# A one-layer decoder step on one core: what ScalarE waits for between two expert products, and how the output is finished and scaled

## The chip, the cores and the metric

The kernel runs on one core of one Trainium2 chip. The metric is the device time of one execution in microseconds (us). The engines are called by the names that the profile uses: PE (TensorE matmul), PEld (its weight loads), DVE (VectorE), ACT (ScalarE), POOL (GpSimd), SP (SyncE, which issues the weight stream). ACTq is the part of ACT that issues DMAs.

## What is computed

288 tokens (256 of a prompt, 8 x 4 of running samples) of width 2048 go through one layer: adaLN modulation, a mixer of an RG-LRU branch and a pooling branch, and an expert layer with 16384 experts. The part that matters here is the end of the expert layer and of the model:

```python
act = jax.nn.gelu(jnp.einsum('td,ted->te', xb, eu[ib]))   # the u product
return jnp.einsum('te,ted->td', wb * act, ev[ib])          # the v product
...
x = x + g2[:, None] * peer(...)                            # residual with a gate
y = rmsnorm(x, final_g)                                    # over the 2048 features
```

The kernel computes both expert products densely: all 16384 experts for all 288 tokens, with the chosen experts' gates written into a mostly zero matrix that is multiplied onto the gelus.

## The kernel before

Features lie on partitions, as 16 chunks of 128; tokens are columns, so a full activation is 128 x 16 x 288. Every float32 weight tile of 128 x 2048 (a unit) comes through one stream into four `raw` buffers and is split in two: ACT rounds it to `w_hi` (line 984 or 992, the functions `hi` and `hi_next`), DVE subtracts to get `w_lo` (lines 484 and 491, `lo` and `lo_next`). Both have two buffers (`SPL = 2`). PE then does three products for a unit: `w_hi` with the high and with the low part of the activation (the hi part of a unit), and `w_lo` with the high part (its lo part). PE signals `pe_hi` after a hi part and `pe_unit` after a unit. ACT may overwrite a `w_hi` buffer after `pe_hi` of the unit two before.

The program runs through the modulation and mixer, the queries, 128 u units and then 128 v units. In the u part ACT turns each unit's result into gelus and stores them, in 16 groups of eight units, to a scratch tensor in DRAM (`store_gelus`, line 1146). The staging tile of these gelus is the same memory as `acc`, in which the v part later sums. In the v part, group g multiplies the gelus and gates of eight units by eight v tiles; each v unit k of a group makes two feature chunks, c = 2k (complete with `vhalf_done`) and c = 2k + 1 (complete with `pe_unit`). They lie in four PSUM banks in turn, and DVE adds them to `acc[:, c]` (line 930; line 928 copies in the first group). Between these, DVE and ACT prepare the next group: `gated` multiplies gelus by gates, ACT rounds (line 1173), DVE subtracts (line 887). ACT also loads gates (line 1164) and gelus (line 1168) of a later group.

Order on each engine is the order in which the code is written; engines meet only through semaphores. At the passage from u to v, ACT stores the last group of gelus, waits until all 16 stores have landed (`gelu_out`), loads gelus 1, gates 2 and gelus 2, and only then rounds the weights of the second v unit. DVE waits for the same stores before its first instruction of the v part.

The last group is unrolled. In it DVE finishes chunks as well: for each unit it makes `w_lo` of the next, adds both chunks, and then runs `finish` for both: `residual` (lines 717, 720, 722) puts the gated sum onto `x`, `add_square` (lines 726, 727) adds the square to a running sum in `rstd`. ACT in this group only rounds weights. After the last chunk DVE copies the sum (line 955), PE adds over partitions (line 1271), ACT takes the square root (line 997), DVE inverts it (line 523) and scales 16 chunks by `final_g` and by the inverse (line 958). After every four chunks SP writes a quarter of the output (line 413).

Of the kernel before, what the change touches and what calls it, by code (L numbers as in the profile page):

```python
# [9 lines left out]
ALU = mybir.AluOpType  # L10
ACT = mybir.ActivationFunctionType
# [3 lines left out]
P = 128  # L15
D = 2048
DC = D // P
SEQ = 256
NB, NS = 8, 4
T = SEQ + NB * NS  # L20
# [41 lines left out]
EG = 8  # L62
NG = P // EG
# [46 lines left out]
NQ = 4  # L110
# [8 lines left out]
def v_unit(g):  # L119
    return V0 + EG * g  # L120
# [36 lines left out]
class Chain:  # L157
# [12 lines left out]
    def link(self, ins):  # L170
        self.done(ins)
        self.wait()
# [26 lines left out]
def hybrid_step(nc, w_stream, vecs_d, c_d, hist_d, x_d, lruw_d, poolw_d, keys_d,  # L199
                o_y, o_conv, o_lru, o_pool):  # L200
    ctx = ExitStack()
    with ctx:
        def sb(name, shape, dt=F, scope=None):
            return (scope or ctx).enter_context(nc.sbuf_tensor(name, shape, dt))

        def sem(name):
            return ctx.enter_context(nc.semaphore(name))
# [7 lines left out]
        x = sb("x", [P, DC, T])  # L215
# [8 lines left out]
        rstd = sb("rstd", [P, 2, T])  # L224
# [16 lines left out]
        acc = sb("acc", [P, DC, T])  # L241
# [5 lines left out]
        def bank(b, n=512, at=0):  # L247
            return ps[:, b * 512 + at:b * 512 + at + n]

        def vec(name):  # L250
            o, w = VOFF[name]
            return vecs[:, o:o + w]
# [118 lines left out]
        gelu_out = [sem("gelu_out0"), sem("gelu_out1")]  # L371
# [4 lines left out]

        vbank_free = [sem(f"vbank{b}_free") for b in range(4)]
        out_ready = sem("out_ready")
        out_sem = sem("out_sem")
        dve_steps, act_steps, pool_steps = sem("dve_steps"), sem("act_steps"), sem("pool_steps")  # L380

# [90 lines left out]
        def _(dve):  # L472
            ch = Chain(dve, dve_steps)
            link = ch.link
            V = nc.vector

            def lo(u):
                if plain(u):
                    return
                s, old = place(u) % SPL, split_before(u)  # L480
                dve.wait_ge(hi_ready, place(u) + 1)
                if old is not None:
                    dve.wait_ge(pe_unit, old + 1)
                V.tensor_tensor(w_lo[:, s, :], raw[:, u % RAW, :], w_hi[:, s, :].bitcast(F), ALU.subtract).then_inc(lo_ready, 1)  # L484
# [212 lines left out]
            for u in range(2 * DC, O0):  # L697
                lo(u + 1)
                kind = ORDER[u - 1]
                if kind[0] == "z" and kind[1] < 16:  # L700
                    n = kind[1]
# [5 lines left out]
                k = ORDER[u - 3]  # L707
# [6 lines left out]
            def residual(c, src, m):  # L714

                xs = x[:, c, SEQ:T].rearrange("p (b t) -> p b t", t=NS)
                V.scalar_tensor_tensor(out=x[:, c, 0:SEQ], in0=src[:, 0:SEQ], scalar=mod[:, m, c, 0:1],
                                       in1=x[:, c, 0:SEQ], op0=ALU.mult, op1=ALU.add)
                tmp = rstd[:, 1, 0:NB * NS].rearrange("p (b t) -> p b t", t=NS)
                link(V.tensor_tensor(tmp, src[:, SEQ:T].rearrange("p (b t) -> p b t", t=NS),  # L720
                                     mod[:, m, c, 1:].unsqueeze(2).to_broadcast([P, NB, NS]), ALU.mult))
                return V.tensor_tensor(xs, xs, tmp, ALU.add)

            def add_square(c, square):

                link(V.tensor_tensor(square, x[:, c, :], x[:, c, :], ALU.mult))
                link(V.tensor_tensor(rstd[:, 0, :], rstd[:, 0, :], square, ALU.add))
# [16 lines left out]
            for u in range(Q0 + 3, Q0 + 8):  # L744
                lo(u + 1)
                kind, n = QORDER[u - Q0 - 1]
# [128 lines left out]
            def gated(tile, g, k, par, turn):  # L875

                if k == 0:
                    dve.wait_ge(gate_in[par], turn)
                    dve.wait_ge(gelu_in[par], turn)
                src = gel_in(g)  # L880
                at_least(dve, gw_ready, tile - 1)
                V.tensor_tensor(prod[:, k % 2, :].rearrange("p (c t) -> p c t", t=TCH), src[:, k, :].rearrange("p (c t) -> p c t", t=TCH),  # L882
                                gates_in[:, par, :, k * TCH:(k + 1) * TCH], ALU.mult).then_inc(prod_done, 1)

            def gated_low(tile, k, par):
                dve.wait_ge(gwhi_ready, tile + 1)
                V.tensor_tensor(gw_lo[:, par, k, :], prod[:, k % 2, :], gw_hi[:, par, k, :].bitcast(F),
                                ALU.subtract).then_inc(gw_ready, 1)

            steps, left = choose(), 0.0  # L890
            for n in range(P):
                now[0] = n
                lo(M0 + n + 1)
                if GATE0_AT <= n < GATE0_AT + EG:
                    k = n - GATE0_AT
# [10 lines left out]
                    left -= cost  # L906
            assert next(steps, "end") == "end" and made["ones", NBT - 1] + 2 < GATE0_AT - 3

            for h in range(2):
                dve.wait_ge(gelu_out[h], 16 * (NG // 2))  # L910

            def v_group(lo_of, tile, par, turn, unit, units, uses, last=None):

                start = isinstance(uses, int) and uses == 0
                if not start:
                    for b in range(4):
                        dve.wait_ge(vbank_free[b], uses)
                for k in range(EG):
                    lo_of(k)
                    for j in TILES[k] if last is None else ():  # L920
                        gated(tile + j, 2 - par, j, par, turn)
                    dve.wait_ge(vhalf_done, units + (k + 1))
                    for h in range(2):
                        c = 2 * k + h
                        if h == 1:
                            dve.wait_ge(pe_unit, unit + (k + 1))
                        if start:
                            n = V.tensor_copy(acc[:, c, :], bank(2 + c % 4, T))
                        else:
                            n = V.tensor_tensor(acc[:, c, :], acc[:, c, :], bank(2 + c % 4, T), ALU.add)  # L930
                        n.then_inc(vbank_free[c % 4], 1)
                    for j in TILES[k] if last is None else ():
                        gated_low(tile + j, j, par)
                    if last:
                        last(2 * k)
                        last(2 * k + 1)

            v_group(lambda k: lo(v_unit(0) + k + 1), EG, 1, 16, v_unit(0), 0, 0)
            with dve.Fori(0, NG // 2 - 1) as i:
                for j in range(2):  # L940
# [5 lines left out]
            def finish(c):  # L946

                dve.wait_ge(vbank_free[c % 4], (NG - 1) * DC // 4 + c // 4 + 1)
                link(residual(c, acc[:, c, :], 5))
                add_square(c, prod[:, 0, :])  # L950

            dve.wait_ge(gw_ready, NG * EG)
# [1 line left out]
            v_group(lambda k: lo(v_unit(g) + k + 1) if k < EG - 1 else None, 0, 0, 0, v_unit(g), g * EG, g * DC // 4, last=finish)  # L954
            V.tensor_copy(prod[:, 1, :], rstd[:, 0, :]).then_inc(sq_ready, 1)
            inv_std(5, rstd[:, 0, :])
            for c in range(DC):
                n = V.scalar_tensor_tensor(out=acc[:, c, :], in0=x[:, c, :], scalar=vec("final")[:, c:c + 1],  # L958
                                           in1=rstd[:, 0, :], op0=ALU.mult, op1=ALU.mult)
                if c % (DC // NQ) == DC // NQ - 1:  # L960
                    n.then_inc(out_ready, 1)


        @block.scalar
        def _(act):
# [9 lines left out]
            def hi(u):  # L975

                if plain(u):
                    return
                s, old = place(u) % SPL, split_before(u)
                act.wait_ge(raw_in[u % RAW], 16 * (u // RAW + 1))  # L980
                if old is not None:
                    act.wait_ge(pe_hi, place(old) + 1)
                    low_made(old)
                nc.scalar.activation(w_hi[:, s, :], raw[:, u % RAW, :], ACT.Copy).then_inc(hi_ready, 1)  # L984
# [95 lines left out]
            for u in range(2 * DC, O0):  # L1080
# [5 lines left out]
                if kind[0] == "z" and kind[1] >= 16:  # L1086
                    n = kind[1]
# [5 lines left out]
                k = ORDER[u]  # L1093
# [109 lines left out]
                if GATE0_AT <= n < GATE0_AT + EG:  # L1203
                    gated_high(n - GATE0_AT, n - GATE0_AT, 0)

            for h in range(2):
                act.wait_ge(gelu_out[h], 16 * (NG // 2))
            act.wait_ge(pe_unit, V0)
            load_gelus(1, gel_in(1), 1)

            def v_group(hi_of, tile, load, par):

                act.wait_ge(gw_ready, tile)
                load()
                for k in range(EG):
                    hi_of(k)
                    for j in TILES[k]:
                        gated_high(tile + j, j, par)

            def load_next(g, h):  # L1220
                return lambda: (load_gates(g, h), load_gelus(g, gel_in(2 - h), h))

            v_group(lambda k: hi(v_unit(0) + k + 1), EG, load_next(2, 0), 1)
            with act.Fori(0, NG // 2 - 2) as i:
                for j in range(2):
                    g = 1 + j

                    def load():
                        if j == 0:
                            load_gates(i * 2 + 3, 1)  # L1230
                            load_gelus(i * 2 + 3, gel_in(1), 1)
                        else:
                            load_gates(i * 2 + 4, 0)
                            load_gelus(i * 2 + 4, gel_in(2), 0)
                    v_group(lambda k: hi_next(v_unit(g), i, 2 * EG, k), i * (2 * EG) + (g + 1) * EG, load, j)
# [1 line left out]
            v_group(lambda k: hi(v_unit(g) + k + 1), (g + 1) * EG, load_next(g + 2, 1), 0)  # L1237
            g = NG - 2
            v_group(lambda k: hi(v_unit(g) + k + 1), (g + 1) * EG, lambda: None, 1)
            for k in range(EG - 1):  # L1240
                hi(v_unit(NG - 1) + k + 1)

            stats(5, rstd[:, 0, :], D, 6)

# [265 lines left out]
```

## Time and profile before

| | |
|---|---|
| median of 3 runs | 2378.15 us (2377.18 to 2379.47) |
| the profiled execution, its own time | 2377.09 us |
| its span, first to last instruction | 2375.1 us |
| PE busy | 2247.8 us, 95% |
| DVE busy | 1381.4 us, 58% |
| ACT busy | 831.8 us, 35% |
| mean granted TensorE clock | 0.971 |

The span is some 2 us shorter than the execution's own time, which includes what lies around the first and the last instruction. Busy shares are means over stages with different limits. In a timeline row the first number is the start in us from the span's start, the second the duration; what stands in brackets is how long the engine sat idle before the row and who ended that.

### The profile page before, as it was taken

The page shows a single profiled execution, that of the slowest core. Times are in us where ns is not written, and L with a number is a line of the kernel's source. Part 1 is how long each engine was busy: PE and PEld are TensorE (multiplying, and loading weights), DVE is VectorE, ACT ScalarE, POOL GpSimd, SP SyncE. Part 2 cuts the span into 40 slices and gives each one's busy share as a digit, 9 for nine tenths or more (in the row PEclk, how much of TensorE's full clock was granted, in tenths as well). Part 3 has the DMA queues.
Part 4 walks back from the last instruction along what each step waited for, and adds up shares of the span by engine and source line. Part 5 has one row for each costly group of instructions (what it writes and reads, how often), then busy time and mean ns, then how long its engine had stood idle before and what let it go on. Part 6 is the DMA issues. An engine that isn't in the chain of part 4 may idle for free.

```text
span 2375.1 us, 38461 instructions
## 1 busy us (share of the span) xinstructions
PE 2247.8 (95%) x16551; PEld 2129.1 (90%) x16551; DVE 1381.4 (58%) x1909; ACT 831.8 (35%) x727; POOL 18.6 (1%) x60
## 2 busy tenths in 40 slices
PE   5599968979999999999999999899999999999997
PEld 0198747968899999999999999899999999999996
DVE  3336546663478886677663334365665566656668
ACT  0222243222333333445543333333333333333331
POOL 0000000000000000000000000000000000000000
PEclk8799988989999999999999999999999999999998
DMA  9967766447644555555555557655555655555542
GB/s 404 380 260 299 269 277 246 161 160 277 228 172 180 184 182 196 199 200 221 212 211 200 188 192 254 213 209 206 210 199 206 233 213 201 199 205 210 199 159 79
DMA packets 105843, 515.93 MB, mean 217 GB/s; under 512 B 8448, under 2 KB 45696, under 8 KB 46464
## 3 DMA queue, kind: packets, MB, share of 16 engines
q1 hardware_dynamic: 59616, 430.35, 48.8%
q10 hardware_dynamic: 45968, 82.17, 9.4%
q8 instruction: 90, 1.47, 0.2%
q0 software_dynamic: 144, 1.73, 0.2%
q14 instruction: 25, 0.20, 0.0%
HBM read 471.92 MB, written 41.99 MB: 216 GB/s over the span
## 4 chain that ended last, share of the span: by engine, by line
PE 90%; DMA 4%; DVE 3%; ACT 1%; issue 1%; ACTq 0%; SPq 0%; DVEq 0%
PE ps L1258 17%; PE ps L1259 16%; PE ps L1264 16%; PE ps L1425 12%; PE ps L1424 11%; PE ps L1432 11%; DMA raw<-in_w_stream_dram 4%; PE ps L1395 3%; PE ps L1283 2%; PE ps L1271 1%; PE ps L1372 0%; DVE mix L502 0%; ACT w_hi L984 0%; DVE act_lo L511 0%; DVE acc L958 0%
## 5 line engine op out<-in xcount | busy, mean ns | idle before, releaser
L1258 PE MATMUL ps<-act_hi,w_hi 128*128 128x288 f32 x2944 | 806.0, 301 | 28.1 <-ACT w_hi L984 14.5
L1259 PE MATMUL ps<-act_lo,w_hi 128*128 128x288 f32 x2944 | 799.6, 298 | 0.0
L484 DVE TENSOR_TENSOR w_lo<-raw,w_hi 128x2048 fp32r<-128x2048 f32 x188 | 430.6, 2291 | 391.2 <-ACT w_hi L984 372.2
L1258 PEld LDWEIGHTS ps<-act_hi,w_hi 128*128 128x128 f32 x2944 | 559.9, 190 | 45.9 <-issue 40.8
L1424 PE MATMUL ps<-gw_hi,w_hi 128*128 128x288 f32 x2048 | 554.4, 297 | 7.7 <-ACT w_hi L984 7.7
L1259 PEld LDWEIGHTS ps<-act_lo,w_hi 128*128 128x128 f32 x2944 | 559.5, 190 | 0.1
L1425 PE MATMUL ps<-gw_lo,w_hi 128*128 128x288 f32 x2048 | 554.7, 298 | 0.0
L984 ACT ACTIVATE w_hi<-raw 128x2048 fp32r<-128x2048 f32 x192 | 367.4, 1914 | 230.6 <-DMA raw<-in_w_stream_dram 103.7
L1264 PE MATMUL ps<-act_hi,w_lo 128*128 128x288 f32 x2944 | 420.8, 295 | 0.1
L1264 PEld LDWEIGHTS ps<-act_hi,w_lo 128*128 128x128 f32 x2944 | 401.3, 189 | 0.3 <-DVE w_lo L484 0.3
L1424 PEld LDWEIGHTS ps<-gw_hi,w_hi 128*128 128x128 f32 x2048 | 386.3, 189 | 7.9 <-ACT w_hi L984 7.9
L1425 PEld LDWEIGHTS ps<-gw_lo,w_hi 128*128 128x128 f32 x2048 | 387.9, 189 | 0.0
L992 ACT ACTIVATE w_hi<-raw 128x2048 fp32r<-128x2048 f32 x120 | 229.9, 1916 | 206.5 <-PE ps L1425 84.2
L491 DVE TENSOR_TENSOR w_lo<-raw,w_hi 128x2048 fp32r<-128x2048 f32 x124 | 283.5, 2286 | 32.1 <-ACT w_hi L992 27.9
L1432 PE MATMUL ps<-gw_hi,w_lo 128*128 128x288 f32 x2048 | 293.9, 296 | 0.0
L1432 PEld LDWEIGHTS ps<-gw_hi,w_lo 128*128 128x128 f32 x2048 | 280.2, 188 | 0.0
L930 DVE TENSOR_TENSOR acc<-acc,ps 128x288 f32<-128x288 f32 x240 | 108.4, 454 | 285.9 <-PE ps L1432 285.9
L1141 ACT ACTIVATE acc<-ps 128x288 f32<-128x288 f32 x128 | 52.6, 411 | 495.5 <-PE ps L1264 495.5
L1173 ACT ACTIVATE gw_hi<-prod 128x288 fp32r<-128x288 f32 x128 | 55.7, 444 | 378.4 <-DVE prod L882 377.9
L1283 PE MATMUL ps<-raw,csil 128*32 128x512 f32 x768 | 119.9, 720 | 51.8 <-DMA raw<-in_w_stream_dram 45.2
L1283 PEld LDWEIGHTS ps<-raw,csil 128*32 128x32 f32 x768 | 18.1, 116 | 127.1 <-DMA raw<-in_w_stream_dram 100.0
L1156 ACT ACTIVATE mix<-ps 128x512 f32<-128x512 f32 x72 | 70.7, 1092 | 2.1 <-PE ps L1395 2.1
(166 smaller groups left out, 937.6 us busy)
## 6 DMA issues: line engine op xcount, KB each, us to landing
raw<-in_w_stream_dram SPq DMA_DIRECT2D x408, 1024.0 KB, 4.9
gelus<-acc ACTq DMA_DIRECT2D x16, 1152.0 KB, 6.6
gates_dense<-mix ACTq DMA_DIRECT2D x18, 1024.0 KB, 4.5
gates_in<-gates_dense ACTq DMA_DIRECT2D x16, 1152.0 KB, 6.6
act_hi<-gelus ACTq DMA_DIRECT2D x15, 1152.0 KB, 11.5
x<-in_x_dram ACTq DMA_DIRECT2D x1, 2304.0 KB, 15.5
out_dram<-acc SPq DMA_DIRECT2D x4, 576.0 KB, 2.8
out_dram<-mix POOLq DMA_DIRECT2D x1, 1692.0 KB, 8.7
```

Source lines behind the costliest of these rows:

```text
L484: V.tensor_tensor(w_lo[:, s, :], raw[:, u % RAW, :], w_hi[:, s, :].bitcast(F), ALU.subtract).then_inc(lo_ready, 1)
L491: V.tensor_tensor(w_lo[:, s, :], raw[:, n % RAW, :], w_hi[:, s, :].bitcast(F), ALU.subtract).then_inc(lo_ready, 1)
L930: n = V.tensor_tensor(acc[:, c, :], acc[:, c, :], bank(2 + c % 4, T), ALU.add)
L984: nc.scalar.activation(w_hi[:, s, :], raw[:, u % RAW, :], ACT.Copy).then_inc(hi_ready, 1)
L992: nc.scalar.activation(w_hi[:, place(n) % SPL, :], raw[:, n % RAW, :], ACT.Copy).then_inc(hi_ready, 1)
L1258: mm(bank(b, T), w_hi[:, s, w], act_hi[:, c, :], start=c == 0, stop=False)
L1259: n = mm(bank(b, T), w_hi[:, s, w], act_lo[:, c, :], start=False, stop=False)
L1264: n = mm(bank(b, T), w_lo[:, s, w], act_hi[:, c, :], start=False, stop=c == DC - 1)
L1283: n = mm(bank(4 + m % 2)[CPAD * b:CPAD * (b + 1), :], csil[:, k, :], raw[:, u % RAW, b * 512:(b + 1) * 512], start=k == 0, stop=k == DC - 1)
L1424: mm(bank(2 + b, T), w_hi[:, s, w], gw_hi[:, par, e, :], start=e == 0, stop=False)
L1425: n = mm(bank(2 + b, T), w_hi[:, s, w], gw_lo[:, par, e, :], start=False, stop=False)
L1432: n = mm(bank(2 + b, T), w_lo[:, s, w], gw_hi[:, par, e, :], start=False, stop=e == EG - 1)
```

## The change

Three edits.

1. At the passage, ACT's wait for all gelu stores becomes a wait for the first store of odd groups (`gelu_out[1]` at 16), which is that of group 1, the one that it loads next. The wait for all stores moves behind ACT's first v group, ahead of the loop. On DVE it moves from ahead of the v part to just ahead of the first copy into `acc`.
2. In the last group DVE calls `finish` for a chunk right behind that chunk's own sum, not for both chunks behind both sums. `finish` signals ACT through a new semaphore, `xnew_ready`, once the chunk's new `x` is written.
3. ACT, in the last group, scales each finished chunk by `final_g` into `acc` (a Copy with a scale per partition) and signals `xg_ready`. At the very end DVE multiplies four quarters of 128 x 1152 by the inverse, in place of 16 chunks of 128 x 288 with two factors.

```diff
-            for h in range(2):
-                dve.wait_ge(gelu_out[h], 16 * (NG // 2))
-
             def v_group(lo_of, tile, par, turn, unit, units, uses, last=None):
...
                         if start:
+                            if c == 0:
+                                for b in range(2):
+                                    dve.wait_ge(gelu_out[b], 16 * (NG // 2))
                             n = V.tensor_copy(acc[:, c, :], bank(2 + c % 4, T))
                         else:
                             n = V.tensor_tensor(acc[:, c, :], acc[:, c, :], bank(2 + c % 4, T), ALU.add)
                         n.then_inc(vbank_free[c % 4], 1)
+                        if last:
+                            last(c)
                     for j in TILES[k] if last is None else ():
                         gated_low(tile + j, j, par)
-                    if last:
-                        last(2 * k)
-                        last(2 * k + 1)
-
...
                 dve.wait_ge(vbank_free[c % 4], (NG - 1) * DC // 4 + c // 4 + 1)
-                link(residual(c, acc[:, c, :], 5))
+                residual(c, acc[:, c, :], 5).then_inc(xnew_ready, 1)
+                dve.wait_ge(xnew_ready, c + 1)
                 add_square(c, prod[:, 0, :])
...
-            for c in range(DC):
-                n = V.scalar_tensor_tensor(out=acc[:, c, :], in0=x[:, c, :], scalar=vec("final")[:, c:c + 1],
-                                           in1=rstd[:, 0, :], op0=ALU.mult, op1=ALU.mult)
-                if c % (DC // NQ) == DC // NQ - 1:
-                    n.then_inc(out_ready, 1)
+            for q in range(NQ):
+                n = DC // NQ
+                c = slice(q * n, (q + 1) * n)
+                dve.wait_ge(xg_ready, (q + 1) * n)
+                V.tensor_tensor(acc[:, c, :], acc[:, c, :], rstd[:, 0, :].unsqueeze(1).to_broadcast([P, n, T]),
+                                ALU.mult).then_inc(out_ready, 1)
...
-            for h in range(2):
-                act.wait_ge(gelu_out[h], 16 * (NG // 2))
+            act.wait_ge(gelu_out[1], 16)
             act.wait_ge(pe_unit, V0)
             load_gelus(1, gel_in(1), 1)
...
             v_group(lambda k: hi(v_unit(0) + k + 1), EG, load_next(2, 0), 1)
+            for h in range(2):
+                act.wait_ge(gelu_out[h], 16 * (NG // 2))
...
-            for k in range(EG - 1):
-                hi(v_unit(NG - 1) + k + 1)
+            for k in range(EG):
+                if k < EG - 1:
+                    hi(v_unit(NG - 1) + k + 1)
+                for c in (2 * k, 2 * k + 1):
+                    act.wait_ge(xnew_ready, c + 1)
+                    nc.scalar.activation(acc[:, c, :], x[:, c, :], ACT.Copy, scale=vec("final")[:, c:c + 1]).then_inc(xg_ready, 1)
```

How ACT's instructions stand at the passage, before. The first row is the last unit's gelu, `gelus<-acc` the last store, the last row the weights of the second v unit; semaphores that a row waits for stand in brackets.

```order
L1141 ACTIVATE acc<-ps 128x288 [waits pe_unit]
L1146 DMA gelus<-acc 128x2304 [waits bank1_free,bank0_free]
L1168 DMA act_hi<-gelus 128x2304 [waits pe_unit,gelu_out1,gelu_out0]
L1164 DMA gates_in<-gates_dense 128x18x128 [waits gw_ready]
L1168 DMA act_hi<-gelus 128x2304
L984 ACTIVATE w_hi<-raw 128x2048 [waits lo_ready,pe_hi,raw_in1]
```

The same place now (line numbers are one higher):

```order
L1142 ACTIVATE acc<-ps 128x288 [waits pe_unit]
L1147 DMA gelus<-acc 128x2304 [waits bank1_free,bank0_free]
L1169 DMA act_hi<-gelus 128x2304 [waits pe_unit,gelu_out1]
L1165 DMA gates_in<-gates_dense 128x18x128 [waits gw_ready]
L1169 DMA act_hi<-gelus 128x2304
L985 ACTIVATE w_hi<-raw 128x2048 [waits lo_ready,pe_hi,raw_in1]
```

No row moved: one semaphore is gone from the first load, and the other is waited for at a lower value. All three loads still stand ahead of the weights.

How ACT's program ends, before: the weights of the last three units, and the square root.

```order
L984 ACTIVATE w_hi<-raw 128x2048 [waits lo_ready,pe_hi,raw_in1]
L984 ACTIVATE w_hi<-raw 128x2048 [waits lo_ready,pe_hi,raw_in2]
L984 ACTIVATE w_hi<-raw 128x2048 [waits lo_ready,pe_hi,raw_in3]
L997 ACT_TABLE_LOAD
L997 ACTIVATE rstd<-ps,epsc 128x288 [waits stat_ready]
```

And now:

```order
L985 ACTIVATE w_hi<-raw 128x2048 [waits lo_ready,pe_hi,raw_in2]
L1247 ACTIVATE acc<-x,vecs 128x288 [waits xnew_ready] x2
L985 ACTIVATE w_hi<-raw 128x2048 [waits lo_ready,pe_hi,raw_in3]
L1247 ACTIVATE acc<-x,vecs 128x288 [waits xnew_ready] x4
L998 ACT_TABLE_LOAD
L998 ACTIVATE rstd<-ps,epsc 128x288 [waits stat_ready]
```

Two scaled copies, each with a wait for DVE, stand between the weights of one unit and of the next; the table load now stands behind the last of them.

How DVE's instructions of one unit stand in the last group, before:

```order
L484 TENSOR_TENSOR w_lo<-raw,w_hi 128x2048 [waits pe_unit,hi_ready,dve_steps]
L930 TENSOR_TENSOR acc<-acc,ps 128x288 [waits vhalf_done]
L930 TENSOR_TENSOR acc<-acc,ps 128x288 [waits pe_unit]
L717 SCALAR_TENSOR_TENSOR x<-acc,mod,x 128x256 [waits vbank0_free]
L720 TENSOR_TENSOR rstd<-acc,mod 128x32
L722 TENSOR_TENSOR x<-x,rstd 128x32 [waits dve_steps]
L726 TENSOR_TENSOR prod<-x 128x288 [waits dve_steps]
L727 TENSOR_TENSOR rstd<-rstd,prod 128x288 [waits dve_steps]
L717 SCALAR_TENSOR_TENSOR x<-acc,mod,x 128x256 [waits vbank1_free,dve_steps]
```

And now, up to the second chunk's residual:

```order
L485 TENSOR_TENSOR w_lo<-raw,w_hi 128x2048 [waits pe_unit,hi_ready,dve_steps]
L931 TENSOR_TENSOR acc<-acc,ps 128x288 [waits vhalf_done]
L718 SCALAR_TENSOR_TENSOR x<-acc,mod,x 128x256 [waits vbank0_free]
L721 TENSOR_TENSOR rstd<-acc,mod 128x32
L723 TENSOR_TENSOR x<-x,rstd 128x32 [waits dve_steps]
L727 TENSOR_TENSOR prod<-x 128x288 [waits xnew_ready]
L728 TENSOR_TENSOR rstd<-rstd,prod 128x288 [waits dve_steps]
L931 TENSOR_TENSOR acc<-acc,ps 128x288 [waits pe_unit,dve_steps]
L718 SCALAR_TENSOR_TENSOR x<-acc,mod,x 128x256 [waits vbank1_free]
```

The second sum moved behind the first chunk's residual and square; `w_lo` of the next unit is still the first of a unit's instructions.

## Rows read from the trace of the kernel before

**Rows 1.** The page's chain that ended last, by engine

```profile
PE 90%; DMA 4%; DVE 3%; ACT 1%; issue 1%; ACTq 0%; SPq 0%; DVEq 0%
```

**Rows 2.** Timeline of ACT at the passage (start, duration, engine, line, what)

```profile
1524.81 0.35 ACTq L1146 DMA_DIRECT2D gelus<-acc  x1
1530.45 0.35 ACTq L1168 DMA_DIRECT2D act_hi<-gelus  x1
1530.84 0.45 ACTq L1164 DMA_DIRECT2D gates_in<-gates_dense  x1
1531.32 5.01 ACTq L1168 DMA_DIRECT2D act_hi<-gelus  x1
1536.45 1.91 ACT L984 ACTIVATE w_hi<-raw 128x2048 fp32r<-128x2048 f32 x1 [11.72 <-issue]
```

**Rows 3.** Timeline of PE at the passage

```profile
1528.41 2.29 PE L1432 MATMUL ps<-gw_hi,w_lo 128*128 128x288 f32 x16
...
1538.41 0.61 PE L1424 MATMUL ps<-gw_hi,w_hi 128*128 128x288 f32 x1 [7.71 <-ACT w_hi L984]
...
1545.42 2.29 PE L1432 MATMUL ps<-gw_hi,w_lo 128*128 128x288 f32 x16
```

**Rows 4.** Timeline of ACT one group later: a gelu load behind a gate load

```profile
1581.42 2.37 ACTq L1168 DMA_DIRECT2D act_hi<-gelus  x1
```

**Rows 5.** Stretches: us; busy of PE, PEld, DVE, ACT, POOL; clock; DMA; GB/s

```profile
226.30:230.70 4.40, 0.06 (x4) 0.00 (x0) 0.02 (x1) 1.91 (x1) 0.00 (x0) 0.94 1.00 421
230.80:233.80 3.00, 3.00 (x13) 3.00 (x14) 2.73 (x2) 1.91 (x1) 0.00 (x0) 0.53 1.02 431
...
262.80:264.50 1.70, 0.22 (x5) 0.17 (x2) 1.70 (x3) 0.73 (x1) 0.00 (x0) 1.00 1.00 352
...
2367.60:2374.30 6.70, 0.00 (x0) 0.00 (x0) 4.30 (x11) 0.00 (x0) 0.00 (x0) 0.50 0.85 352
```

**Rows 6.** Timeline of PE in the last group: lo parts of its units 0 and 1

```profile
2309.39 2.30 PE L1432 MATMUL ps<-gw_hi,w_lo 128*128 128x288 f32 x16
...
2315.81 2.30 PE L1432 MATMUL ps<-gw_hi,w_lo 128*128 128x288 f32 x16
```

**Rows 7.** Timeline of DVE in the last group, its units 0 and 1

```profile
2310.66 0.46 DVE L930 TENSOR_TENSOR acc<-acc,ps 128x288 f32<-128x288 f32 x1 [2.26 <-PE ps L1432]
2311.73 0.46 DVE L930 TENSOR_TENSOR acc<-acc,ps 128x288 f32<-128x288 f32 x1 [0.61 <-PE ps L1432]
...
2312.94 0.46 DVE L726 TENSOR_TENSOR prod<-x 128x288 f32<-128x288 f32 x1
...
2313.93 0.48 DVE L717 SCALAR_TENSOR_TENSOR x<-acc,mod,x 128x256 f32<-128x256 f32 x1
...
2315.76 2.29 DVE L484 TENSOR_TENSOR w_lo<-raw,w_hi 128x2048 fp32r<-128x2048 f32 x1
2317.97 0.81 DVE L930 TENSOR_TENSOR acc<-acc,ps 128x288 f32<-128x288 f32 x2
```

**Rows 8.** Timeline of ACT: an activation of 288 columns and the next instruction

```profile
1492.66 0.44 ACT L1173 ACTIVATE gw_hi<-prod 128x288 fp32r<-128x288 f32 x1
1492.99 1.91 ACT L984 ACTIVATE w_hi<-raw 128x2048 fp32r<-128x2048 f32 x1
```

**Rows 9.** Timeline of ACT at the end: table load and square root

```profile
2343.67 1.28 ACT L997 ACT_TABLE_LOAD   x1
2362.43 0.50 ACT L997 ACTIVATE rstd<-ps,epsc 128x288 f32<-128x288 f32 x1 [17.47 <-PE ps L1271]
```

**Rows 10.** Timeline of DVE at the end: last sum, copy, scaling

```profile
2356.66 0.46 DVE L930 TENSOR_TENSOR acc<-acc,ps 128x288 f32<-128x288 f32 x1 [0.54 <-PE ps L1432]
...
2360.70 0.31 DVE L955 COPY prod<-rstd 128x288 f32<-128x288 f32 x1
...
2364.95 6.96 DVE L958 SCALAR_TENSOR_TENSOR acc<-x,vecs,rstd 128x288 f32<-128x288 f32 x16
```

**Rows 11.** Timeline of DVE earlier: a quarter of 1152 columns by a broadcast factor

```profile
490.65 1.36 DVE L499 TENSOR_TENSOR mix<-x,rstd 128x1152 f32<-128x1152 f32 x1
```

More of the change, by code:

```diff
@@ L378, in hybrid_step @@
         out_ready = sem("out_ready")
+        xnew_ready, xg_ready = sem("xnew_ready"), sem("xg_ready")
         out_sem = sem("out_sem")
```

## The prediction, made before the changed kernel had run

> **What bounds the kernel now.** I read the chain that ended last, then the timelines of ACT, PE and DVE where the diff touches them. The chain is PE for 90% of the span [rows 1], and nearly all of that is matmuls behind matmuls, which the change doesn't touch. So only two places can move the time: the passage, where PE stands still, and the end, where PE is done and DVE, ACT and the output DMA stand in the chain.
>
> At the passage PE ends the first v unit 2.14 us into its lo part, at 1530.6, and stands for 7.71 us until ACT has rounded the second unit's weights [rows 3]. ACT is free of gelus when it issues the last store at 1524.81, issues the next DMA at 1530.45 (when the store has landed), and then sits 5.01 us in the issue of gelus 2; only then come the weights, at 1536.45 [rows 2]. The stall has a tail: the next hi part takes 1538.41 to 1545.42, 7.01 us [rows 3], against 2/3 of a 6.42 us unit, 4.28 [rows 6]: 2.73 us more, at the lower granted clock. The passage thus costs 10.4 us.
>
> In the last group a unit takes PE 6.42 us [rows 6]. DVE is as full: `w_lo` (2.21 from its start to the next instruction), two sums and two finishes, 6.59 us in all [rows 7]. ACT has slack there.
>
> **Edit 1, the passage.** The wait for the store goes, and what is late next is the issue of gelus 2, which stays ahead of the weights. With a gate load alone ahead, such an issue takes 2.37 us [rows 4]; with gelus 1 ahead as well, 5.01 [rows 2]. So one 1152 KB transfer ahead costs 2.64. Now the last store (also 1152 KB) is ahead too: 2.37 + 2 x 2.64 = 7.65. The three issues now start right behind the store's, at 1525.2; gelus 2 at about 1526.0 (0.35 and 0.45 for the two before it), held to 1533.7. I take 1534.0, since the store also shares the engines with a weight load. Before it ended at 1536.33. The stall shrinks by 2.3 us, to 5.4. Bounds: no gain, if the loads are held until the store has landed all the same; 7.7, if the store and gelus 1 don't hold the issue at all.
>
> The clock's tail: a stretch of 4.4 us without work on PE, earlier in the trace, is followed by 3.0 us at a granted clock of 0.53, in which 13 matmuls run [rows 5] where 6.42 / 48 = 0.134 each would give 22: 9 x 0.134 = 1.2 us lost. After 7.71 us it is 2.73. For 5.4 us I take 2.0, so 0.7 is gained, between 0 and 1.5. **Edit 1: 3.0 us gained** (0 to 10.4). DVE's moved wait costs nothing: its first copy into `acc` comes after the weights in any case, and the store has landed by then. The wait behind ACT's first v group comes some 50 us (8 x 6.42) after the store.
>
> **Edits 2 and 3, the last group.** ACT's program now has two scaled copies between the weights of one unit and of the next. So the weights of unit k + 1 wait for the new `x` of chunk 2k - 1, which DVE makes after unit k - 1 is complete; and DVE's `w_lo` waits for those weights and stands ahead of the next sums. That closes a ring through both engines. One turn, from the sum of a unit's second chunk: 1.21 until its `x` is written (2311.73 to 2312.94); the copy; 1.91 for the weights [rows 2]; 0.04 to DVE; 2.21 for `w_lo`; 2.20 for sum and finish of the first chunk (2311.73 to 2313.93) [rows 7]. The copy: an activation of 288 columns holds ACT 0.33 [rows 8], one with a pointer operand runs 0.50 [rows 9]; I take 0.40. Sum: 7.97 us, against PE's 6.42: 1.55 more per unit, once the slack is used.
>
> The slack, in the clock times of before: the first sum is at 2310.66 [rows 7], the second 2.20 later at 2312.86, its `x` at 2314.07, the copy ends at 2314.47, weights of unit 2 are ready at 2316.38. PE wants them when unit 1 ends, at 2315.81 + 2.14 = 2317.95 [rows 6]: in time. One turn on, unit 3's weights are ready at 2324.35, wanted at 2324.37: just in time. Unit 4's at 2332.32, wanted at 2330.79: 1.53 late. Each further turn adds 1.55, so unit 7 starts 1.53 + 3 x 1.55 = 6.2 us late. Behind it DVE makes `w_lo` of unit 7 (from 2356.27), then chunks 12 to 15 at 2.20 each, and reaches the copy of the sum at 2367.3, where it was at 2360.70 [rows 10]: **6.6 us lost**. With a copy of 0.33 or 0.50 the turn is 7.90 or 8.07 and the loss 6.1 or 7.2.
>
> **Edit 3, the tail.** Sixteen scalings take 6.96 us, so the first quarter is out after four of them, about 1.8 us [rows 10]. A quarter by a broadcast factor takes 1.36 [rows 11], so the first write starts 0.45 sooner and the last quarter is done some 1.8 sooner. But the four writes fill 0.85 of the DMA engines' 6.7 us [rows 5], so they can close up by 1.0 at most: 1.45. I take **1.4 gained** (0.5 to 1.8). The table load, until now far ahead of its use [rows 9], moves behind the last copy. From the last sum ACT needs 1.21 + 0.45 + 1.28 = 2.9 us to have it; DVE and PE need 2.20 + 1.73 = 3.9 to bring ACT its input (1.73 from DVE's copy to the square root [rows 9, 10]). So it hides with 1 us to spare.
>
> The Trainium skill (ScalarE: Activation LUTs, What ACT_TABLE_LOAD costs) gives a switch of tables 1.28 us and a drain of 1.38 on top, about 2.66 in all. The row has the 1.28; nothing stood behind it that would show a drain. By the page the table would be there 4.3 us after the last sum, 0.4 after the input, and the sum below would be 0.4 higher.
>
> **The sum.** -3.0 + 6.6 - 1.4 = +2.2 us. On the profiled execution's 2377.09 that is 2379.3. It lies 1.06 under the median of 2378.15, so the time to expect of a median is 2380.3. A measurement of this kernel can tell about 0.2%, 4.8 us, so this is no change that it can show: two opposite effects of several us.
>
> **The rivals.**
> *The issue isn't held.* If gelus 2 is taken without the queue having to drain, the weights come at about 1526.8, before PE wants them: no stall, no low clock, 10.4 gained in place of 3.0. Net -5.2: 2373.0. For it: the store itself takes 0.35 to issue [rows 2]. Against it: every gelu load behind a gate load is held over 2 us, and longer with more ahead [rows 2, 4]. The Trainium skill (DMA: Bandwidth & Descriptors, Queues, rings and completion order) says that an engine takes a ring's descriptors in order. By that rule the gate load can't pass the store, and this rival falls.
> *The hold ends no earlier.* If the loads' data moves only once the store has landed, ACT is free at 1536.3 as before, and the end alone counts: +5.2, 2383.3, slower. For it: no row shows a load issued behind a store in flight. It decides where edit 1 gains under 0.4.
> *The clock falls in the last group.* Slower, too: PE now stands four times for 1.5 us. An earlier stretch of 1.7 us in which PE worked 0.22 kept 1.00 [rows 5]; if a row of such stalls doesn't, a unit costs 1.2 to 2.7 more. Up to 1.55 that hides in the ring's turn, except in the last unit; at 2.73 it is 3 x 1.18 + 2.73 = 6.3 more, 2386.6. It passes the bound from about 1.8 a unit.
> *The ring doesn't form.* If the weights don't wait for the copies, PE keeps its pace, chunk 14 is finished while chunk 15 is summed, the copy of the sum is 0.7 earlier and the tail 1.4: -3.0 - 2.1 = -5.1, 2373.1. The order of ACT's rows speaks against it.
>
> **How the numbers follow.** My forecast has 0.70 (2377.5 to 2383), the issue not held 0.08, the hold as long as before 0.10, the clock 0.08, no ring 0.04. The range leaves out the two fast rivals and the clock at its worst: 2375.5 to 2384.0. Faster by over 0.2%: the two fast rivals, less the part that ends short of it, 0.10. Slower: the hold as before, half of the clock, and a small edge of my forecast where the copy takes 0.5 and the tail gains little, 0.20. Within: 0.70.
>
> **What would show it.** At the passage: the issue of gelus 2 held about 8 us and ending near 1534, PE's stall near 5.4, and a low clock after it. In the last group: weights on ACT no longer released by PE but behind the scaled copies; PE with stalls of about 1.5 before units 4 to 7; DVE idle about 1.5 before each `w_lo`. At the end: four instructions of about 1.36, writes nearly back to back, the table load clear of the square root. I am wrong if PE shows no stalls in the last group, or if the one at the passage is gone or unchanged.

## The result: slower by 0.22%, in three parts

The changed kernel takes 2385.26 us (median of 13 runs, 2382.49 to 2387.95), the kernel before 2380.61 us (median of 13 runs, 2377.18 to 2382.59). The ratio is 1.0022, with a 95% interval of 1.0013 to 1.0030: some 5.2 us slower. (The ratios here are estimated from all runs and need not equal the quotient of the two medians, which differ by 4.65.) The prediction took 0.2% for the least that a measurement of this kernel can tell; the interval, 0.0009 to either side, is narrower than that and excludes a ratio of 1. The forecast was +2.2 us and 2380.3 us, with a range of 2375.5 to 2384.0. The direction of each part was right, the sum was not, and the time lies outside the range.

One table holds nearly everything that follows. Each profiled execution is cut at two instructions of DVE: the first sum of the last group and the copy of the sum of squares. A is the time from the issue of the last gelu store to that first sum (the passage and the v groups), B from there to the copy (the last group), C from the copy to the end of the span (the tail). The rows of before are [rows 2, 7, 10], with its span (2375.13 to the hundredth); the others are worked out in the same way from their own timelines.

| kernel | A | B | C | ratio to before |
|---|---|---|---|---|
| before | 785.85 | 50.04 | 14.44 | |
| changed | 783.23 | 59.03 | 13.16 | 1.0022 (1.0013 to 1.0030) |
| e1, passage alone | 783.89 | 50.04 | 14.44 | 0.9987 (0.9978 to 0.9996) |
| e2, end alone | 784.80 | 59.05 | 13.16 | 1.0034 (1.0023 to 1.0044) |
| e3, no copies on ACT | 783.21 | 50.39 | 14.41 | 0.9988 (0.9979 to 0.9997) |
| e4, copies one unit later | 783.48 | 50.39 | 13.16 | 0.9991 (0.9982 to 1.0000) |
| e5, gates loaded last | 775.30 | 59.03 | 13.13 | 0.9988 (0.9979 to 0.9997) |
| e8, loads behind the weights | 780.09 | 59.02 | 13.15 | 0.9995 (0.9986 to 1.0004) |
| e9, sums first | 782.70 | 57.73 | 13.15 | a single run |
| e6, three things mended | 776.58 | 49.65 | 13.15 | 0.9954 (0.9941 to 0.9968) |

So the change gives 2.62 us in A, takes 8.99 in B and gives 1.28 in C: +5.1 us in the two profiled executions. (Their spans differ by 8.3; the other 3.2 lie ahead of the last gelu store, in code that the change doesn't touch.)

**The passage (A).** ACT's timeline at the passage, against [rows 2]:

```profile
1527.97 0.35 ACTq L1147 DMA_DIRECT2D gelus<-acc  x1
1528.41 0.39 ACTq L1169 DMA_DIRECT2D act_hi<-gelus  x1
1528.84 1.29 ACTq L1165 DMA_DIRECT2D gates_in<-gates_dense  x1
1530.16 7.49 ACTq L1169 DMA_DIRECT2D act_hi<-gelus  x1
1537.77 1.91 ACT L985 ACTIVATE w_hi<-raw 128x2048 fp32r<-128x2048 f32 x1 [9.89 <-issue]
```

The wait for the store is gone, and the time is spent in the issue of gelus 2 instead: 7.49 us where it was 5.01. The weights start 9.8 us after the store's issue, where it was 11.6. PE's timeline shows the rest, against [rows 3]:

```profile
1531.56 2.29 PE L1439 MATMUL ps<-gw_hi,w_lo 128*128 128x288 f32 x16
...
1539.74 0.61 PE L1431 MATMUL ps<-gw_hi,w_hi 128*128 128x288 f32 x1 [5.88 <-ACT w_hi L985]
```

The stall is 5.88 us, where it was 7.71. The stretches say what the clock did (length; busy us of PE, PEld, DVE, ACT, POOL with instructions; granted clock; DMA share; GB/s):

```profile
1533.85:1539.74 5.89, 0.01 (x2) 0.01 (x1) 0.02 (x1) 1.91 (x1) 0.00 (x0) 0.77 1.08 340
1539.74:1546.00 6.26, 6.26 (x33) 6.26 (x34) 5.41 (x8) 2.62 (x3) 0.00 (x0) 0.67 0.90 346
```

The granted clock fell during the stall, as before, and 33 matmuls took 6.26 us, 1.8 more than 33 x the 0.134 that one takes at the upper level.

**The last group (B).** DVE's timeline over one unit, against [rows 7]:

```profile
2313.53 0.45 DVE L931 TENSOR_TENSOR acc<-acc,ps 128x288 f32<-128x288 f32 x1
2314.01 0.48 DVE L718 SCALAR_TENSOR_TENSOR x<-acc,mod,x 128x256 f32<-128x256 f32 x1
...
2314.86 0.46 DVE L727 TENSOR_TENSOR prod<-x 128x288 f32<-128x288 f32 x1
...
2317.29 2.29 DVE L485 TENSOR_TENSOR w_lo<-raw,w_hi 128x2048 fp32r<-128x2048 f32 x1 [1.48 <-ACT w_hi L985]
2319.50 0.45 DVE L931 TENSOR_TENSOR acc<-acc,ps 128x288 f32<-128x288 f32 x1
...
2321.82 0.45 DVE L931 TENSOR_TENSOR acc<-acc,ps 128x288 f32<-128x288 f32 x1
```

ACT's timeline beside it:

```profile
2314.86 0.54 ACT L1247 ACTIVATE acc<-x,vecs 128x288 f32<-128x288 f32 x1 [1.79 <-DVE x L723]
2315.30 1.90 ACT L985 ACTIVATE w_hi<-raw 128x2048 fp32r<-128x2048 f32 x1
2320.83 0.54 ACT L1247 ACTIVATE acc<-x,vecs 128x288 f32<-128x288 f32 x1 [3.63 <-DVE x L723]
```

That is the ring. DVE sums the second chunk of a unit at 2313.53 and has its `x` at 2314.86; ACT copies and reaches the weights at 2315.30; DVE, idle for 1.48 us, makes `w_lo` at 2317.29 and sums the next second chunk at 2321.82: 8.29 us a turn of the ring, against 6.42 on PE. PE's timeline shows what that does to it (a few matmuls of the group; in brackets the stall):

```profile
2325.55 0.40 PE L1431 MATMUL ps<-gw_hi,w_hi 128*128 128x288 f32 x1 [0.49 <-ACT w_hi L985]
...
2333.84 0.40 PE L1431 MATMUL ps<-gw_hi,w_hi 128*128 128x288 f32 x1 [1.60 <-ACT w_hi L985]
...
2342.13 0.40 PE L1431 MATMUL ps<-gw_hi,w_hi 128*128 128x288 f32 x1 [1.60 <-ACT w_hi L985]
...
2350.42 0.40 PE L1431 MATMUL ps<-gw_hi,w_hi 128*128 128x288 f32 x1 [1.61 <-ACT w_hi L985]
```

These are the stalls before units 3 to 6; the one before unit 7 is 1.60. Over the whole stretch B the granted clock stays at 1.00:

```profile
2311.20:2370.23 59.03, 47.29 (x344) 45.88 (x342) 47.60 (x103) 19.83 (x23) 0.00 (x0) 1.00 0.14 52
```

**The tail (C).** DVE's and ACT's ends, against [rows 9, 10]:

```profile
2369.80 1.28 ACT L998 ACT_TABLE_LOAD   x1
2371.96 0.50 ACT L998 ACTIVATE rstd<-ps,epsc 128x288 f32<-128x288 f32 x1 [0.88 <-PE ps L1278]
```

```profile
2370.23 0.31 DVE L955 COPY prod<-rstd 128x288 f32<-128x288 f32 x1
...
2374.48 5.16 DVE L961 TENSOR_TENSOR acc<-acc,rstd 128x1152 f32<-128x1152 f32 x4
```

From the copy to the first scaling it is 4.25 us in both kernels; the scaling itself takes 5.16 us where it took 6.96, and the span ends 1.28 sooner after the copy. The four writes now run at 0.96 of the DMA engines, where it was 0.85 [rows 5]:

```profile
2376.60:2382.60 6.00, 0.00 (x0) 0.00 (x0) 3.04 (x3) 0.00 (x0) 0.00 (x0) 0.50 0.96 393
```

### The profile page after: what moved, and what is told of

It is laid out like the page before. It is cut to its first block, busy times and chain, and to the rows that moved or that the text cites. A ratio compares the mean times of both kernels' runs of the same rounds, so it can differ in the third digit from the quotient of the medians.

```text
span 2383.4 us, 38467 instructions
## 1 busy us (share of the span) xinstructions
PE 2251.8 (94%) x16551; PEld 2130.6 (89%) x16551; DVE 1380.6 (58%) x1897; ACT 840.1 (35%) x743; POOL 18.8 (1%) x60
## 4 chain that ended last, share of the span: by engine, by line
PE 88%; DVE 5%; DMA 4%; ACT 2%; issue 1%; ACTq 1%; DVEq 0%; SPq 0%
PE ps L1265 17%; PE ps L1266 16%; PE ps L1271 16%; PE ps L1432 11%; PE ps L1431 11%; PE ps L1439 11%; DMA raw<-in_w_stream_dram 4%; PE ps L1402 3%; PE ps L1290 2%; ACT w_hi L985 1%; DVE w_lo L485 1%; PE ps L1278 1%; PE ps L1379 0%; DVE mix L503 0%; DVE x L718 0%
## 6 DMA issues: line engine op xcount, KB each, us to landing
act_hi<-gelus ACTq DMA_DIRECT2D x15, 1152.0 KB, 11.5
```

## Experiments

### The two halves apart

e1 has the passage edit alone, e2 the end alone.

```diff
 e1 (the kernel before):
-            for h in range(2):
-                act.wait_ge(gelu_out[h], 16 * (NG // 2))
+            act.wait_ge(gelu_out[1], 16)
 (DVE's wait moved to its first copy into acc, ACT's behind its first v group)
 e2 (the changed kernel): the same lines the other way round
```

> The kernel before with the passage edit alone. In the trace of the changed kernel the stall at the passage is 5.88 us against 7.71, and the low clock behind it costs some 0.8 us less. Theory (the store in front of the three loads holds their issue, so only a part of the stall goes): 2.6 us faster than before, ratio 0.9989, stall on PE between 5.4 and 6.4 us. Rival (the gain shows only because the stages ahead ran otherwise in that execution): stall within 0.3 us of 7.7, no gain. Rival (the issue isn't held): no stall, 10.4 us faster, ratio 0.9956.

Measured: ratio 0.9987, 3.1 us faster (the interval allows 1.0 to 5.2). PE's stall:

```profile
1541.31 0.61 PE L1425 MATMUL ps<-gw_hi,w_hi 128*128 128x288 f32 x1 [6.15 <-ACT w_hi L984]
```

B and C are those of before to the hundredth. The theory holds: a part of the stall goes, not all of it. The stall is 1.56 us shorter than in the profile of before, and A is 1.96 shorter; the other 0.4 lies behind the stall, at the low clock.

> The kernel before with the edits of the last group and the tail alone. Theory (a ring through ACT and DVE of 8.3 us a unit against PE's 6.42): PE stalls of about 1.6 us before units 4 to 7 and a smaller one before unit 3, copy of the sum about 9 us later, writes done 1.2 us sooner after it; 7.8 us slower than before, ratio 1.0033. Rival (the two parts are not independent, and what the passage gives is taken back at the end): between 4 and 6 us slower.

Measured: ratio 1.0034, 8.1 us slower (5.5 to 10.5). B is 59.05, C 13.16, those of the changed kernel; the waits of the stretch have the same five PE stalls (engine, for whom: us in total, times, longest):

```profile
DVE w_lo L485 <- ACT w_hi L985: 8.9, 6, 1.5
...
PE ps L1430 <- ACT w_hi L985: 6.9, 5, 1.6
```

The halves are independent: 0.9987 x 1.0034 = 1.0021, against 1.0022 of both. The interval (5.5 to 10.5 us) alone would not rule out the upper end of the rival's 4 to 6; B and C in the trace do. One thing beside: with the passage of before, A is 784.80 here and 785.85 in the profile of before, so the same code at the same place differs by 1 us between executions: 0.2 in the stall (7.49 here, 7.71 there), the rest behind it. By the table, the passage edit is worth 0.9 to 3.2 us, depending on which two executions one compares.

### What closes the ring

e3 takes ACT's copies away; e4 keeps them and puts them one unit later; e9 keeps them in place and restores the order of the sums.

```diff
 e3 (the changed kernel):
-            for k in range(EG):
-                if k < EG - 1:
-                    hi(v_unit(NG - 1) + k + 1)
-                for c in (2 * k, 2 * k + 1): ... (wait and scaled copy)
+            for k in range(EG - 1):
+                hi(v_unit(NG - 1) + k + 1)
 (and the sixteen scalings of before on DVE)
 e4 (the changed kernel):
+            def scaled(k): ... (the waits and copies of chunks 2k and 2k + 1)
             for k in range(EG):
                 if k < EG - 1:
                     hi(v_unit(NG - 1) + k + 1)
-                for c in (2 * k, 2 * k + 1): ...
+                if k:
+                    scaled(k - 1)
+            scaled(EG - 1)
 e9 (the changed kernel): finish(2k) and finish(2k + 1) behind both sums
```

> The changed kernel without the scaled copies on ACT: weights alone on ACT in the last group, sixteen scalings on DVE at the end as before; each chunk is still finished behind its own sum. Theory (the ring through ACT is what costs): no PE stall in the last group, a DVE turn of 2.21 + 2 x 2.32 = 6.85 us, copy of the sum 0.3 us later than before relative to the group's start; with the passage 2.3 us faster than before, ratio 0.9990. Rival (the new order of finishing costs, since each residual now waits for its own sum to end): PE stalls stay, 5 us or more slower than before.

Measured: ratio 0.9988, 2.9 us faster than before. PE waits for nobody in the last group, and DVE runs without a gap; two turns of its timeline:

```profile
2317.04 2.29 DVE L485 TENSOR_TENSOR w_lo<-raw,w_hi 128x2048 fp32r<-128x2048 f32 x1
2319.25 0.45 DVE L931 TENSOR_TENSOR acc<-acc,ps 128x288 f32<-128x288 f32 x1
2321.56 0.45 DVE L931 TENSOR_TENSOR acc<-acc,ps 128x288 f32<-128x288 f32 x1
2323.89 2.29 DVE L485 TENSOR_TENSOR w_lo<-raw,w_hi 128x2048 fp32r<-128x2048 f32 x1
```

A turn is 6.85 us (2317.04 to 2323.89), as expected, and B 50.39, 0.35 over before. The copies close the ring, not the order of finishing.

> The changed kernel with ACT's scaled copies one unit later: the copies of a unit's two chunks stand behind the weights of the unit after next, not ahead of them. Nothing is left out. Theory (the ring is closed by the place of the copies, not by their cost): no PE stall in the last group, DVE turn 6.85 us, the tail 1.2 us shorter; 3.5 us faster than before, ratio 0.9985. Rival (ACT's or DVE's added work itself is too much, or the copies disturb DVE): a turn over 7.2 us and PE stalls, slower than before.

Measured: ratio 0.9991, 2.1 us faster than before, with an interval (0.0 to 4.3 us) that takes in the 3.5 expected. In the trace B is 50.39 and C 13.16: the full gain of the tail, and the loss of the last group gone. The same sixteen copies run on ACT, and its weights are released by PE again. The copies of chunks 0 and 1 now stand ahead of the weights of unit 3; in the changed kernel they stood ahead of those of unit 2:

```profile
2315.42 0.54 ACT L1245 ACTIVATE acc<-x,vecs 128x288 f32<-128x288 f32 x1 [1.79 <-DVE x L723]
2317.16 1.92 ACT L985 ACTIVATE w_hi<-raw 128x2048 fp32r<-128x2048 f32 x1 [1.20 <-PE ps L1437]
```

So the copies cost nothing by themselves. What cost 8.6 us (59.03 to 50.39) was their place ahead of the next weights.

> The changed kernel with both sums ahead of both finishes again; ACT's scaled copies stay where they are. Theory (the ring is closed by the copies' place; the order of finishing only sets its length): PE stalls stay in the last group, a turn of 0.73 + 1.83 + 0.84 + 0.44 + 1.91 + 0.04 + 2.21 = 8.0 us against 8.29, stalls of about 1.3 us, 1.5 to 2 us less lost than in the changed kernel. Rival (finishing behind each chunk's own sum closes the ring): no PE stall in the last group.

Measured in a single run, so the trace counts more than its time. The stalls stay, a little shorter, by the waits of the last group:

```profile
DVE w_lo L485 <- ACT w_hi L986: 8.9, 6, 1.5
...
PE ps L1432 <- ACT w_hi L986: 6.2, 5, 1.4
```

`w_lo` stands at 2316.16, 2324.20, 2332.24: a turn of 8.04, as worked out. B is 57.73, 1.3 less than in the changed kernel, where 1.5 to 2 were expected. The start takes some of it back. DVE now sums both chunks of unit 0 before it finishes either, and stands 0.61 us for the second:

```profile
2310.69 0.46 DVE L931 TENSOR_TENSOR acc<-acc,ps 128x288 f32<-128x288 f32 x1 [0.61 <-PE ps L1440]
...
2316.16 2.29 DVE L485 TENSOR_TENSOR w_lo<-raw,w_hi 128x2048 fp32r<-128x2048 f32 x1 [1.48 <-ACT w_hi L986]
```

From the group's first sum to this `w_lo` it takes 6.54 us, where it was 6.09: 0.45 more. The five turns that follow give 1.24, and the last unit gives 0.51 (10.98 from its `w_lo` to the copy of the sum, where it was 11.49). The order of finishing sets the ring's length, and doesn't close it.

### What holds ACT at the passage

e5 exchanges two DMAs, e8 puts the weights ahead of both.

```diff
 e5 (the changed kernel):
-            v_group(..., EG, load_next(2, 0), 1)
+            v_group(..., EG, lambda: (load_gelus(2, gel_in(2), 0), load_gates(2, 0)), 1)
 e8 (the changed kernel), in ACT's first v group:
                 for k in range(EG):
                     hi_of(k)
+                    if k == 0:
+                        load()
```

> The changed kernel with two DMAs at the passage exchanged: gelus 2 is loaded ahead of gates 2. Nothing is left out. Theory (what holds ACT is the DMA right behind a gate load, whose 512 B pieces are made only as the queue drains; with the gate load last nobody stands behind it): the weights of the second v unit start within 4 us of the store's issue (9.7 in the changed kernel), PE's stall there is under 1 us and the clock stays; 7 us faster than the changed kernel, 2.5 us faster than before, ratio 0.9990. Rival (the queue takes only so many transfers at a time, whatever their pieces): ACT is held 6 us or more all the same, stall on PE over 3 us, no gain on the changed kernel.

Measured: ratio 0.9988 to before, 2.9 us faster, while B is still 59.03. ACT's timeline:

```profile
1527.41 0.35 ACTq L1147 DMA_DIRECT2D gelus<-acc  x1
1527.86 2.29 ACTq L1169 DMA_DIRECT2D act_hi<-gelus  x2
1530.18 0.85 ACTq L1165 DMA_DIRECT2D gates_in<-gates_dense  x1
1531.15 1.92 ACT L985 ACTIVATE w_hi<-raw 128x2048 fp32r<-128x2048 f32 x1 [3.83 <-issue]
```

The same four transfers are taken in 3.6 us, and the weights start 3.7 us after the store's issue. PE has no stall at the passage at all, and the clock stays. A is 775.30, 7.9 less than in the changed kernel and 10.5 less than before: the whole passage, as it was priced. The rival falls: the queue takes four transfers in 3.6 us. What is held for long is the DMA behind a gate load. Why that is so (by the expectation, pieces that are made only as the queue drains) this run doesn't show.

> The changed kernel with the weights of the second v unit put ahead of the loads of gates 2 and gelus 2 (gelus 1 stays ahead). Theory: the weights start about 1.5 us after the store's issue and PE doesn't stall at this unit, whatever holds the loads; but ACT is then held by gelus 2 until some 10 us after the store's issue and DVE's first gated products wait for gelus 1, so the third unit's weights come about when PE wants them: stall there between 0 and 2 us. 6 to 7.5 us faster than the changed kernel, ratio to before 0.9990 to 0.9995. Rival (what PE saves at the second unit it loses at the third): stalls of 4 us or more there, no gain.

Measured: ratio 0.9995; A is 780.09, 3.1 less than in the changed kernel, half of what was expected. ACT's and PE's timelines:

```profile
1527.11 1.91 ACT L985 ACTIVATE w_hi<-raw 128x2048 fp32r<-128x2048 f32 x1 [1.10 <-issue]
1527.13 1.05 ACTq L1165 DMA_DIRECT2D gates_in<-gates_dense  x1
1528.21 10.60 ACTq L1169 DMA_DIRECT2D act_hi<-gelus  x1
1538.86 0.78 ACT L1174 ACTIVATE gw_hi<-prod 128x288 fp32r<-128x288 f32 x2 [9.83 <-issue]
1539.54 1.89 ACT L985 ACTIVATE w_hi<-raw 128x2048 fp32r<-128x2048 f32 x1
```

```profile
1541.49 0.42 PE L1434 MATMUL ps<-gw_hi,w_hi 128*128 128x288 f32 x1 [3.08 <-ACT w_hi L985]
```

The second unit's weights are early, and the hold falls on the third unit's: 10.60 us, longer than the 7.49 in the changed kernel. This is the rival's mechanism at three quarters of its size (3.08 for 4 or more), and some gain is left. Why the hold is 3 us longer here wasn't tried, but the trace shows what else ran. From 1535 to 1538, inside the hold, a weight tile takes the DMA engines: SP's queue q1 moves 1.04 MB and ACT's queue q10 only 0.15 (queue: packets, MB, share of 16 engines).

```profile
q1 hardware_dynamic: 139, 1.04, 86.0%
q10 hardware_dynamic: 269, 0.15, 17.1%
```

In the changed kernel's trace the same 3 us, in which its hold ends, have no packet of q1:

```profile
q10 hardware_dynamic: 1291, 1.00, 102.8%
```

The size fits; a run without that tile, which would show it, wasn't made.

### A version that takes both

```diff
 e6 (the changed kernel): e5's order of loads, e4's place of the copies, and
-                        if last:
+                        if last and k == EG - 1:
                             last(c)
...
+                    if last and k < EG - 1:
+                        last(2 * k)
+                        last(2 * k + 1)
```

> The changed kernel with three things mended: gates 2 loaded behind gelus 2, the scaled copies one unit later on ACT, and both sums ahead of both finishes again, except in the last unit. Theory (the parts add up): passage 10 us less than before, copy of the sum 0.4 us earlier, tail 1.2 us shorter: 11.6 us faster than before, ratio 0.9951, no PE stall in the last group and a DVE turn of 6.6 us. Rival (the hold on ACT stays): 4 us faster than before, ratio 0.9983.

Measured: 2367.43 us against 2379.33 of before, ratio 0.9954 (0.9941 to 0.9968): 11 us faster by the ratio. A is 776.58 (a stall of 1.05 us is left before the third unit, whose weights wait behind ACT's gated products), B 49.65, 0.39 under before, C 13.15. The parts add up: -9.3, -0.4 and -1.3. PE's waits in the last stretch are down to the one for DVE's sum:

```profile
PE ps L1286 <- DVE prod L958: 4.1, 1, 4.1
```

## Why the prediction was wrong

**Edit 1: the stall was priced well, the clock's part came out by luck.** Forecast: 3.0 us gained, 2.3 in the stall and 0.7 in the low clock behind it; trace 2.6, of which 1.8 in the stall; e1 3.1. The issue of gelus 2 was forecast to be held about 8 us and to end 9.2 after the store's issue; it was held 7.49 and ended 9.7 after. The pricing of a transfer ahead at 2.64 us from two rows was good enough (the sum of 7.65 stands against 6.3 to 7.8 in the five executions with this order of loads); not foreseen was that the gate load's own issue is held too (1.29 for 0.45). The stall was 5.88 for 5.4. The clock's tail was 1.8 for 2.0, but the rule behind the 2.0, the longer the stall the longer the tail, doesn't hold. After e2's stall of 7.49 us PE does as much as after the changed kernel's 5.88, and after e3's of 5.16 it does less (first e2, then e3, each with the 6.26 us that follow):

```profile
1542.10 0.61 PE L1430 MATMUL ps<-gw_hi,w_hi 128*128 128x288 f32 x1 [7.49 <-ACT w_hi L985]
1542.10:1548.36 6.26, 6.26 (x33) 6.26 (x34) 5.26 (x8) 2.62 (x3) 0.00 (x0) 0.67 1.00 371
...
1540.22 0.61 PE L1426 MATMUL ps<-gw_hi,w_hi 128*128 128x288 f32 x1 [5.16 <-ACT w_hi L984]
1540.22:1546.48 6.26, 6.26 (x28) 6.26 (x29) 5.42 (x8) 2.61 (x3) 0.00 (x0) 0.54 1.04 386
```

What the edit takes off the stall is 1.3 to 2.6 us by these traces; what the clock adds or takes back differs by up to 0.8 between executions. The Trainium skill (Perfetto Trace Analysis, DMA Instruction — HWDGE (DVE, Sync)) says that the interval shown for a DMA's issue contains the wait for the descriptor generator and the making of the descriptors, not the transfer. e5 agrees: the same transfers, in another order, are issued in 3.6 us in place of 9.7.

**The ring was foreseen, and sized too short.** This is the step that failed. The turn was put at 7.97 us and the loss at 6.6; they are 8.29 and 8.99. Forecast and measured, term by term, from the rows above: sum to `x` 1.21 and 1.33 (2313.53 to 2314.86); copy 0.40 and 0.44; weights to `w_lo` 1.95 and 1.99; `w_lo` 2.21 and 2.21; sum and finish of the first chunk 2.20 and 2.32 (2319.50 to 2321.82). Three quarters of it is one cause. In the kernel before, a chunk's residual starts 0.37 us behind a sum [rows 7: 2.20 less the 1.83 of a finish], because that sum is the other chunk's; now it stands behind its own and waits for its end, 0.48 (2313.53 to 2314.01); the wait in the program is the one for `vbank0_free`, which that very sum now signals. e9 bears this out: with the two sums together again, and nothing else changed, the turn is 8.04, shorter by twice 0.12. The prediction took 1.21 and 2.20 from rows in which the two sums stand together, though the change is just that they no longer do. Of the 2.4 us that the loss was too small, six turns of 0.32 are 1.9, and four more chunks outside the turns, at 0.12 each, the rest.

**The slack ran out a unit sooner.** Unit 3's weights were forecast to be just in time; PE stood 0.49 us for them. That is the same cause: one turn of 0.32, and 0.12 twice in the first unit's two finishes ahead of it.

**The tail was right.** 1.4 forecast, 1.28 measured; writes nearly back to back; the table load clear of its use. ACT idled 0.88 us between the end of the load and the square root, and PE's result ended that. The page of the Trainium skill (ScalarE: Activation LUTs, What ACT_TABLE_LOAD costs) that adds a drain of 1.38 us to the load would have put the square root 0.5 later; no such time is in this trace, and the measurement decides.

**The absolute time.** 2380.3 was built on a median of three runs, 2378.15. Thirteen runs of the same kernel, those three among them, gave 2380.61, thirty others 2379.6. So 2.5 of the 5.0 us between forecast and result are the base, and the other 2.5 are the change (4.65 between the two medians, for 2.2). Either error alone would have left the time inside the range. In the profiles, the last gelu store is issued at 1524.81 to 1529.27, though nothing ahead of it differs between these kernels. The range took in the bounds of the terms and left out that spread of 4.5 us.

**The rivals.** The clock kept in the last group (granted 1.00 over B). The issue was held, and ended 9.0 to 10.0 us after the store's in the five executions with this order of loads, where 9.2 was forecast and 11.5 was before. The ring formed. The outcome is the forecast's own mechanism, with the ring's terms too small and the base too low.

## What to carry to other kernels

When an engine that feeds the bottleneck is given work that waits for another engine, write down the closed chain of waits and its length per turn before the work's own cost: here sixteen copies of half a microsecond cost nothing one unit later, and 8.6 us where they stood. A duration read from rows holds for that order of instructions; when the change alters the order, read each gap again with its dependency in mind. A removed wait at a DMA queue may only hand its time to the next issue: look at what is queued behind a transfer of many small pieces, and put that one last.

## What the runs showed of the hardware

- The DMA that is issued right behind a gate load (1152 KB in pieces of 512 B) holds its engine: 1.7 to 3.5 us with nothing else ahead (the groups after the passage, all kernels), 4.8 and 5.0 with one 1152 KB transfer ahead (e2, before), 6.3 to 7.8 with two, 10.6 in e8. A gelu load of the same size in the same queue, with no gate load ahead, is taken in 0.39 us behind one transfer (changed kernel) and in about 1.9 behind two (e5, 2.29 for both).
- The gate load's own issue grows too with what is queued ahead: 0.45 with one 1152 KB transfer ahead (before), 1.25 to 1.95 with two (changed kernel, e1, e3, e4, e9).
- What the low clock costs behind a stall of over 5 us doesn't follow the stall's length. A less the stall, against e5's 775.30 without one, gives 2.8 us after 7.71 (before), 2.0 after 7.49 (e2), 2.1 after 5.88 (changed) and 2.8 after 5.16 (e3).
- Four stalls of 1.6 us, 8.3 us apart, left the granted clock at its upper level, 2.4 GHz (1.00 over B of the changed kernel). The single stalls of 5.2 to 7.7 us at the passage each brought it down to 1.2 GHz (0.50 from 1535 to 1544 in before; 0.54 and 0.67 over the 6.26 us behind e3's and e2's), and 3.1 us in e8 did as well (0.73 over the 6.26 us behind it).
